# Decay exponents spread by loads and a predicated copy; x, B and the modulation sums turned by VectorE blocks

## The reference, cut to what matters

```python
acs = jnp.cumsum(a, axis=2)                       # a = dt * A, per chunk and head
seg = acs[:, :, :, None] - acs[:, :, None, :]
decay = jnp.exp(jnp.where(lower, seg, -jnp.inf))
cb = jnp.einsum('bclgn,bcsgn->bclsg', cm, bm)
y_diag = jnp.einsum('bclsg,bclsgr,bcsgrp->bclgrp', cb, decay, xdt)
...
mod_l = (jax.nn.silu(c) @ w_ada[layer] + b_ada[layer])[:, None, :]
```

## Time and profile before

| | us |
|---|---|
| median of 3 runs | 1884.4 (1882.55 to 1885.38) |
| the profiled execution, its own time | 1884.75 |
| span of the profiled execution | 1882.9 |

### The profile page before, as it was taken

The page is one execution under the profiler, slowest core; times in us unless marked ns, Lnnn a source line. Parts: engine busy times, 40 slices in busy tenths (PEclk is TensorE's granted clock), DMA queues, the critical chain, the costliest instruction groups (busy, mean ns, idle before and its releaser), DMA issues.

```text
span 1882.9 us, 15679 instructions
## 1 busy us (share of the span) xinstructions
PE 1435.3 (76%) x4503; PEld 830.9 (44%) x4503; DVE 1451.5 (77%) x2808; ACT 547.1 (29%) x1558; POOL 855.5 (45%) x626
## 2 busy tenths in 40 slices
PE   7999999999878888887787677677655554655554
PEld 2565687788545555554454234334311111211111
DVE  1545359773797779888967898889989889898877
ACT  3100233432332334223322432233322222222222
POOL 0888410010454443443434455446656555555551
PEclk9999999999989988999889898779878777777876
DMA  9534311343999999999999999999999999999995
GB/s 382 192 147 152 116 65 55 108 176 135 379 393 421 422 421 421 422 421 422 420 421 420 385 399 421 421 423 421 421 421 422 420 422 422 422 422 421 422 422 246
DMA packets 91228, 652.52 MB, mean 347 GB/s; under 512 B 10494, under 2 KB 10886, under 8 KB 12806
## 3 DMA queue, kind: packets, MB, share of 16 engines
q0 software_dynamic: 76448, 555.78, 71.6%
q1 hardware_dynamic: 13808, 93.39, 12.5%
q10 hardware_dynamic: 887, 2.35, 0.3%
HBM read 649.37 MB, written 2.11 MB: 346 GB/s over the span
## 4 chain that ended last, share of the span: by engine, by line
DMA 41%; PE 28%; DVE 20%; issue 6%; ACT 4%; POOL 1%; SPq 0%; DVEq 0%; ACTq 0%; POOLq 0%
DMA arena<-in_peer_uv,arena 40%; PE bank L834 12%; DVE arena L2038 8%; PE bank L1135 4%; DVE arena L2074 4%; PE bank L1023 3%; DMA arena<-in_w_ada 2%; PE bank L871 1%; POOL arena L766 1%; PE bank L948 1%; PE bank L1056 1%; ACT arena L1475 1%; PE bank L974 1%; PE bank L960 1%; DVE arena L2001 1%
## 5 line engine op out<-in xcount | busy, mean ns | idle before, releaser
L766 POOL DMA_INDIRECT arena<-in_peer_uv,arena x512 | 698.1, 1363 | 732.4 <-DVE arena L2074 451.8
L1135 PE MATMUL bank<-arena,smalls 128*128 128x512 f32 x1036 | 660.2, 772 | 419.5 <-ACT smalls L1483 419.4
L2038 DVE CUSTOM_DVE_ANT_0 arena<-arena 128x1024 f32<-128x1024 f32 x512 | 619.1, 1222 | 153.5 <-DMA arena<-in_peer_uv,arena 152.1
L1135 PEld LDWEIGHTS bank<-arena,smalls 128*128 128x128 f32 x1036 | 218.4, 229 | 781.1 <-ACT smalls L1483 589.1
L2074 DVE SCALAR_TENSOR_TENSOR arena<-arena 128x1024 f32<-128x1024 f32 x247 | 315.7, 1278 | 38.9 <-ACT arena L1475 36.3
L834 PE MATMUL bank<-arena 128*128 128x256 f32 (+1 forms) x1216 | 332.0, 430 | 2.2 <-ACT arena L1200 1.5
L1470 ACT ACTIVATE arena<-arena 128x2 f32<-128x2 f32 x255 | 51.9, 203 | 924.7 <-DVE arena L2038 924.6
L834 PEld LDWEIGHTS bank<-arena 128*128 128x128 f32 x1216 | 232.9, 193 | 102.4 <-issue 77.6
L1475 ACT ACTIVATE arena<-arena 128x1 f32<-128x1 f32 x510 | 122.5, 287 | 8.5
L1078 PE MATMUL bank<-arena 128*128 128x256 f32 x480 | 108.8, 380 | 0.0
L1483 ACT ACTIVATE smalls<-ident,arena 128x128 f32<-128x128 f32 x259 | 103.6, 401 | 8.3
(11 more groups left out here) (275 smaller groups left out, 1320.9 us busy)
## 6 DMA issues: line engine op xcount, KB each, us to landing
arena<-in_w_in SPq DMA_DIRECT2D x40, 1024.0 KB, 7.7
arena<-in_w_ada POOLq DMA_DIRECT2D x16, 1024.0 KB, 5.1
arena<-in_w_out SPq DMA_DIRECT2D x16, 1024.0 KB, 9.3
arena<-in_peer_w_q SPq DMA_DIRECT2D x16, 1024.0 KB, 9.3
arena<-in_w_ada SPq DMA_DIRECT2D x8, 1024.0 KB, 12.1
arena<-in_peer_uv,arena POOLq DMA_INDIRECT x512, 19.6
arena<-in_x SPq DMA_DIRECT2D x4, 512.0 KB, 11.9
arena<-in_x_t SPq DMA_DIRECT2D x1, 2048.0 KB, 16.0
```

The source lines that it names most:

```text
L766: nc.gpsimd.indirect_dma_start(gslot[slot], None, uv_tab[0], bass.IndirectOffsetOnAxis(eid[t % 2][:, k:k + 1], 0)).then_inc(s_gsl[slot], 16)
L1135: last = mm(acc[h][:, :], diag[:, k % NDG], row_v(n)[:, h * 512:(h + 1) * 512], start=first, stop=last_one)
L2038: V.tensor_tensor_reduce(row_u(n), row_u(n), h2[t], 1.0, 0.0, ALU.mult, ALU.add, dots[:, k:k + 1]).then_inc(s_dot, 1)
```

## The change

Four things are changed together:

- The exponents. The cumulative sums of the latent chunks are also computed transposed ("acsT": two matmuls, heads on the partitions), copied by ScalarE (`acsr`) and stored to a scratch in DRAM. For each block a load issued from ScalarE's queue spreads the 2 x 512 values of its heads over all 128 partitions (`load_rows`, three buffers `drows`). ScalarE then adds the negated sum of each partition's own token (`log_decays`, again eight instructions, in place), VectorE picks one direction or the other by a predicated copy of 128x512 at the start of `dt_times_cb`, and ScalarE takes the exponential from SBUF. `decay_sums`, its bank and its strict triangles are gone.
- x and B. The 72 transposes on TensorE and their drains are gone. VectorE turns 32x32 blocks from SBUF to SBUF (`turn_blocks`): for every pair of channel tiles 16 instructions on 32 partitions, of 256 elements for the latents and 128 for the context, 192 in all. They are put between the convolutions by `TURN`; the context part of the last three pairs follows after the last convolution, ahead of the dt chain.
- The modulation sums. `ada_sum` is gone; `ada_piece` is a VectorE reduction of 512 elements with a transpose, after every second channel tile, and one matmul by a folding matrix follows after the first z product. GpSimd waits for that reduction where it waited for TensorE. The bias is added by four instructions in place of eight small ones.
- The order. "acsT", "acs" and "m2T" stand between the third and the fourth z product, where they stood after the transposes.

```diff
-        if ct % 2 and ct > 1:
-            plan.append(("ada2", ct // 2 - 1))
-    plan += ["dtl", "dtc", ("ada2", NXB // 2 - 1), ("z", 0, 0), "dt"]
-    plan += [("z", hq, 0) for hq in range(1, 4)]
-    plan += [("xsT", m, h) for m in range(NT) for h in range(2)] + [("bT", m) for m in range(NT)]
-    plan += ["acs", "m2T"]
+    plan += ["dtl", "dtc", ("z", 0, 0), "dt", "ada2"]
+    plan += [("z", 1, 0), ("z", 2, 0), "acsT", "acs", "m2T", ("z", 3, 0)]
...
-        atri = [at(k, HPG * P) for k in (100, 102, 188, 190)]
+        drows = [at(k, 2, HPG * P) for k in (100, 48, 188)]
+        NDR = len(drows)
...
+        NBLK = P // 32
+        apart, fold = at(157, 4 * KD * NBLK), at(157.5, P)
...
-                    await_filled(pool, ("ada2", g - 2))
+                    pool.wait_ge(s_ared, g - 1)
...
+                    ps = claim("ada2")
+                    pe.wait_ge(s_fold, 1)
+                    pe.wait_ge(s_ared, NXB // 2)
+                    filled(mm(ps[:, 0:P], fold, apart, start=True, stop=True), "ada2")
+                if hq == 2:
+                    pe.wait_ge(s_a, 1)
+                    pe.wait_ge(s_const, 4)
+                    ps = claim("acsT")
+                    mm(ps[0:LT * HEADS, 0:P], adec[:, 0, 0:LT].rearrange("p m h -> p (m h)"), upper[:],
+                       start=True, stop=True)
+                    filled(mm(ps[0:LT * HEADS, P:2 * P], adec[:, 1, 0:LT].rearrange("p m h -> p (m h)"), lower[:],
+                              start=True, stop=True), "acsT")
+                    ps = claim("acs")
+                    NSC = NT * HEADS
+                    ad = adec[:].rearrange("p d m h -> p (d m h)")
+                    mm(ps[:, 0:NSC], upper[:], ad[:, 0:NSC], start=True, stop=True)
+                    mm(ps[:, NSC:2 * NSC], lower[:], ad[:, NSC:2 * NSC], start=True, stop=True)
+                    filled(mm(ps[:, 2 * NSC:4 * NSC], ones[:], ad, start=True, stop=True), "acs")
+                    pe.wait_ge(s_mod2, 1)
+                    filled(tr(claim("m2T")[0:4 * KD, 0:P], mod2[:], ident[:]), "m2T")
...
-            await_read(pe, ("bT", NT - 1))
+            pe.wait_ge(s_xtr, N_XTR)
...
-            def decay_sums(mg):
-
-                m, g = mg
-                b = m * NG + g
-                ps = claim(("r", m, g))
-                if b == 0:
-                    pe.wait_ge(s_tri, 4)
-                for d, tri in enumerate((after, before)):
-                    pe.wait_ge(s_atri, (2 * b + d + 1) * HPG)
-                    last = mm(ps[:, :], tri, atri[(2 * b + d) % 4], start=(d == 0), stop=(d == 1))
-                filled(last, ("r", m, g))
...
+            ps = await_bank(act, "acsT")
+            release(A(acsr[0:LT * HEADS].rearrange("p d t -> p (d t)"), ps[0:LT * HEADS, 0:2 * P], ACT.Copy), "acsT")
+            await_read(act, "acsT")
+            act.dma_start(acs_scratch.rearrange("d r t -> r d t"), acsr[0:LT * HEADS]).then_inc(s_acsst, 16)
+            z_gate(3)
+
+            def load_rows(b):
+                act.dma_start(drows[b % NDR], acs_scratch.rearrange("d (b r) t -> d b (r t)", r=HPG)[:, b]
+                              .partition_broadcast(P)).then_inc(s_drow[b % NDR], 16)
+
+            act.wait_ge(s_acsst, 16)
+            load_rows(0)
+            load_rows(1)
...
-                if b == 1:
-                    await_filled(act, ("st", len(steps) - 1, 1))
-                if b >= 2:
-                    await_filled(act, ("r", (b - 2) // NG, (b - 2) % NG))
-                for d, tri in enumerate((upper, lower)):
-                    dst = atri[(2 * b + d) % 4]
+                act.wait_ge(s_drow[b % NDR], 16 * (b // NDR + 1))
+                if b == 0:
+                    act.wait_ge(s_neg, 1)
+                for d in range(2):
                     for r in range(HPG):
-                        h = g * HPG + r
-                        A(dst[:, r * P:(r + 1) * P], tri[:], ACT.Copy, scale=adec[:, d, m, h:h + 1]).then_inc(s_atri, 1)
+                        row = drows[b % NDR][:, d, r * P:(r + 1) * P]
+                        A(row, row, ACT.Identity, bias=adec[:, d, m, g * HPG + r:g * HPG + r + 1]).then_inc(s_ldec, 1)
...
-                    ps = await_bank(act, ("r", m, g))
-                    if b >= 2:
-                        act.wait_ge(s_m, b - 1)
-                    release(A(decay[:, b % 2], ps[:, :], ACT.Exp), ("r", m, g))
-                    if b == 0:
-                        log_decays(1)
+                    act.wait_ge(s_ldsel, b + 1)
+                    A(drows[b % NDR][:, 0], drows[b % NDR][:, 0], ACT.Exp).then_inc(s_dexp, 1)
                     if b + 2 < LT * NG:
-                        log_decays(b + 2)
+                        if b == 0:
+                            await_filled(act, ("st", len(steps) - 1, 1))
+                        else:
+                            act.wait_ge(s_m, b)
+                        load_rows(b + 2)
+                    if b + 1 < LT * NG:
+                        log_decays(b + 1)
...
+            dve.wait_ge(s_const, 1)
+            V.tensor_reduce(out=fold.rearrange("p (a c) -> p a c", a=NBLK),
+                            in_=ident[:].rearrange("p (a c) -> p c a", a=NBLK).unsqueeze(1).to_broadcast([P, NBLK, 32, NBLK]),
+                            axis=mybir.AxisListType.X, op=ALU.add).then_inc(s_fold, 1)
+
             def ada_piece(g):
-                ps = await_bank(dve, ("ada2", g))
-                j = B_BA + 2 * KD + 4 * g
-                release(V.tensor_tensor(modr[:, 4 * g:4 * g + 4], ps[:, 0:4], colB[:, j:j + 4], ALU.add),
-                        ("ada2", g))
-
+                dve.wait_ge(s_asum, g + 1)
+                V.tensor_reduce(out=apart[:, 16 * g:16 * g + 16], in_=asum[:, g % 2].rearrange("p (b r) -> p b r", r=32),
+                                axis=mybir.AxisListType.X, op=ALU.add, apply_transpose=True).then_inc(s_ared, 1)
+
+            def turn_blocks(pair, ctx):
+
+                dve.wait_ge(s_xb, 4 * pair + 4)
+                src = xbc_c if ctx else xbl
+                ct = 2 * pair
+                dst, col = (xs, ct * P) if ct < NX else (Bt, (ct - NX) * P)
+                lo, hi = (LT, NT) if ctx else (0, LT)
+                for a in range(NBLK):
+                    for b in range(NBLK):
+                        i = src[32 * a:32 * a + 32, ct:ct + 2].rearrange("p k (m t) -> p k m t", t=P)
+                        o = dst[32 * b:32 * b + 32, lo:hi, col:col + 2 * P].rearrange("p m (k c) -> p k m c", c=P)
+                        V.transpose(o[:, :, :, 32 * a:32 * a + 32], i[:, :, :, 32 * b:32 * b + 32]).then_inc(s_xtr, 1)
+
+            TURN = {ct: [(ct // 2 - 1, 0)] for ct in range(3, NCTX + 2, 2)}
+            TURN |= {NCTX: [(0, 1)], NXB - 2: [(1, 1)], NXB - 1: [(2, 1)]}
...
+            ada_piece(NXB // 2 - 1)
+            for pair in range(3, NCTX // 2):
+                turn_blocks(pair, 1)
...
+            ps = await_bank(dve, "ada2")
+            for q in range(NBLK):
+                lanes = slice(32 * q, 32 * q + 32)
+                add = V.tensor_tensor(modr[lanes, :], ps[lanes, 0:P].rearrange("p (i q) -> p i q", q=NBLK)[:, :, q],
+                                      colB[lanes, B_BA + 2 * KD:B_BA + 6 * KD], ALU.add)
+                if q < NBLK - 1:
+                    post(add)
+            release(add, "ada2")
...
+            V.tensor_scalar(adec[:], acs[:], -1.0, None, ALU.mult).then_inc(s_neg, 1)
...
+                dve.wait_ge(s_ldec, 2 * HPG * (b + 1))
+                to_end, to_start = (drows[b % NDR][:, d].rearrange("p (r l) -> p r l", l=P) for d in range(2))
+                V.copy_predicated(to_end, lower[:].bitcast(U32).unsqueeze(1).to_broadcast([P, HPG, P]),
+                                  to_start).then_inc(s_ldsel, 1)
...
-                await_read(dve, ("r", m, g))
+                dve.wait_ge(s_dexp, b + 1)
                 settle()
-                V.tensor_tensor(mdec[:, b % 2], mdec[:, b % 2], decay[:, b % 2], ALU.mult).then_inc(s_m, 1)
```

More of the change, by code:

```diff
@@ L835, in project_T @@
                 filled(last, name)
-            def ada_sum(g):
-                ps = claim(("ada2", g))
-                pe.wait_ge(s_asum, g + 1)
-                for j in range(4):
-                    last = mm(ps[:, j:j + 1], asum[:, g % 2, j * P:(j + 1) * P], ones[:, 0:1],
-                              start=True, stop=True)
-                filled(last, ("ada2", g))
             for n in range(XBC // WCOL):
@@ L863, in _ @@
                 filled(last, name)
-            ada_sum(NXB // 2 - 1)
             def z_part(hq, half, i):
@@ L985, in y_transpose @@
                     filled(last, ("yT", m, h))
-            parts = {"proj": proj, "step": step, "cb": c_times_b, "r": decay_sums, "y": diagonal, "off": entering,
+            parts = {"proj": proj, "step": step, "cb": c_times_b, "y": diagonal, "off": entering,
                      "yT": y_transpose}
@@ L1221, in _, with z_gate @@
             A(alog[:], alog[:], ACT.Exp).then_inc(s_dtl, 1)
```

(2 more changed lines are left out.)

73 lines of the change are left out of this document (17 added, 56 removed).

## The result

| | median, us | runs from | to |
|---|---|---|---|
| before, 20 runs | 1883.5 | 1881.24 | 1886.45 |
| changed, 20 runs | 1889.38 | 1884.4 | 1893.95 |
| ratio | 1.0029 | 1.0023 | 1.0036 (95%) |

The changed kernel is 5.9 us slower. So the two traces show 1.9 of the 5.9 us, and what they don't show is taken up at the end.

What follows compares the result with a forecast made beforehand. TensorE, with VectorE as second limit, was taken to bound the part before the gathers, which DMA holds. Terms -9.3, +3.2 and -5.7 made -11.8 us: 1873.0 profiled, 1872.6 median; forecast 1868 to 1879, range 1863 to 1889.

Steps and rivals of the forecast that it cites:

- Price of a transpose: VectorE's block transposes ahead of the states: 0.22 us for 128 elements, 0.35 for 256, putting dt at 227.2 us.
- The rest of the front: From dt to the first state step: log decays, sums 1.3 us, fourth z 7.0, projection 3.5; step at 248.3.
- GpSimd, store and reload, exponentials of the sums at nothing: Ahead of the first state step: these lie beside other work and add nothing; exponentials some 3 us if uncovered.
- Stretch 2: First state step to second block of chunk 1: five predicated copies on a full VectorE, +3.2 us.
- Stretch 3: Second block of chunk 1 to entering states of the last chunk: VectorE paces at 79.1 us, 5.7 us sooner.
- the 4 us of new waits: VectorE's added waits in the later blocks, for ScalarE's loop and TensorE's last application: 4 us, between 0 and 10.
- The row loads: Loads of the sums in the blocks: landing in 4.8 us; rival of late landing decides from 10 us, chance 0.07.
- The sum: Whole kernel: -9.3 + 3.2 - 5.7 = -11.8 us, giving 1873.0 us profiled and a median of 1872.6.
- Each small instruction pays its full duration or a little more: Rival on VectorE's transposes: 0.28 to 0.31 and 0.41 to 0.44 us, costing 7 to 12 us; chance 0.17.
- From +0.1 us per instruction on the gain is eaten: VectorE's transposes behind channel tile 11: 0.1 us more each and the tail eats all of the 11.8 us.
- Two cycles per element: Rival on VectorE's transposes: 0.62 and 0.35 us each, 25 us more, 1898 us in all; chance 0.13.
- the estimate of no gain: From the skill page: transposes at 0.31 and 0.44 us lengthen the tail after channel tile 11 by 11.5 us.

Runs made afterwards that it cites:

- the turns late: Changed kernel with the last 48 of the 96 context transposes moved behind the dt chain and the copies of the sums; 1890.48 us, ratio 1.0038.
- four tiles a turn: Changed kernel with the same elements turned four channel tiles at a time, 96 instructions in place of 192; 1874.1 us, ratio 0.9948.
- the left-out kernel: Changed kernel with 48 of the 96 context transposes left out, so some values differ from the reference; 1869.23 us, ratio 0.9927.
- the version that beats both: Changed kernel with latents turned in 48 instructions of 512 elements and 24 context transposes back on TensorE between second and third z; 1870.31 us, ratio 0.9932.
- the second trace: Changed kernel run again, nothing edited, for another profile; median 1889.85 us, ratio 1.0024, profiled execution 1892.49 us.

## Why the prediction was wrong

- *Price of a transpose: the step that failed.* It took 0.22 and 0.35 us, "near the quick end", from pairs of L1784. Measured 0.333 and 0.464. With 96 and 32 of them behind channel tile 11 that is 96 x 0.113 + 32 x 0.114 = 14.5 us. Up to tile 11 the forecast held (VectorE free at 177.3, measured 177.31; that it is exact is luck, since five other traces with the same work up to there have 176.0 to 179.1), and from there dt came 14.7 late: 241.90 for 227.2. Two points give the law that the prediction lacked: 0.20 us + 1.02 ns per element. The slope was right (it had 1.04), the fixed part was not (0.07). The prediction reasoned that a step is shorter than the duration of one, as with L1784 (0.60 for 0.69). For these transposes it is longer: 0.333 for a mean duration of 0.301, and 0.464 for 0.433. Which of their differences from L1784 does it (the operation, the 32 partitions) no run tells.
- *The rest of the front.* The chain from dt to the log decays took 9.5 (9.2 predicted). The sums took 2.9 (251.43 to 254.34) for 1.3, and the fourth z 7.3 for 7.0: together 1.9 us, which the prediction priced at the full clock though it had itself put an idle TensorE ahead of them. The granted clock was 0.50 in the sums and 0.94 in the fourth z. At 1.00 the sums take 1.6, so 0.3 of it is a short count and not the clock. 14.7 + 0.3 + 1.9 = 16.9; the first step was forecast for 248.3 and came at 265.1.
- *A wait that it did not name.* The fold needs VectorE's last reduction; it had this at 216 and it came at 225.29 (the end of the reductions and turns, late for the same price). Ahead of it stands the wait of 4.12 us for ScalarE, which the prediction did not name either. The second and third z products stand behind both. In the changed kernel that was covered by the later wait of 8.49; in the kernels with dt early it comes to the fore (4.34 us with the turns late, 6.75 with four tiles a turn).
- *GpSimd, store and reload, exponentials of the sums at nothing:* no sign against it; the left-out kernel comes to 250.0 without a term for them. GpSimd's last sum does hold up VectorE's last reduction there, by 0.93 us, and by 5.31 in the version that beats both, but TensorE waits for neither.
- *Stretch 2:* +3.2 predicted, +2.9 measured (265.11 to 340.00, where before took 72.0). It counted five predicated copies up to this mark and eleven behind it; there are six and ten, the sixth at 339.38, so 0.6 us belong to the other stretch and the sum doesn't change. The copies step at 0.63, for 0.65:

```profile
339.38 0.73 DVE L1773 COPY_PREDICATED arena<-early,arena 128x512 f32<-128x512 uint32 x1
340.00 1.28 DVE L1784 TENSOR_TENSOR arena<-arena,smalls 128x512 f32<-128x512 f32 x2
```

- *Stretch 3:* -5.7 predicted, -8.1 measured. The mechanism was right, the 4 us of new waits were too many: they come to 1.6 us. VectorE's waits, 340 to 412 us, beside the earlier trace rows:

```profile
DVE arena L1794 <- DVE arena L1590: 0.5, 1, 0.5
DVE arena L1744 <- PE bank L822: 0.4, 1, 0.4
DVE arena L1764 <- PE bank L905: 0.3, 1, 0.3
DVE arena L1803 <- PE bank L918: 0.2, 1, 0.2
DVE arena L1773 <- ACT arena L1259: 0.2, 1, 0.2
```

- *The row loads.* The rival is out. They land in 4.8 us as taken, and ScalarE waited for them twice, 1.4 us in all (waits, 265 to 417 us):

```profile
arena<-acs_scratch ACTq DMA_DIRECT2D x16, 512.0 KB, 4.8
...
ACT arena L1259 <- DMA arena<-acs_scratch: 1.4, 2, 1.2
```

- *The sum.* 1873.0 + 16.8 (front) - 0.3 - 2.4 (blocks) = 1887.1, and the profiled execution took 1886.6. The median's further 2.8 us are not settled: the second trace shows its own 5.9 us ahead of the gathers and partly ahead of TensorE's first wait, and filling TensorE's waits won nothing clear of it.
- *The rivals.* "Each small instruction pays its full duration or a little more" was the one that happened, 0.02 us beyond its upper end (0.33 and 0.46, for 0.28 to 0.31 and 0.41 to 0.44); its 1880 to 1884 was too low by that and by those 1.9 us, while the blocks gained more than forecast. "From +0.1 us per instruction on the gain is eaten" was right as well. It was given 0.17, with a reason but no row for it; the row against it was of another operation and shape. Two cycles per element is out: the slope is that of L1784.
- The Trainium skill, "VectorE: DVE Perf Modes", sections "The three transpose paths" and "The TRN2 errata", had pointed the right way, against the change: small tiles pay a fixed extra per instruction. The trace agrees: 96 instructions fewer saved 16.1 us. Its 311 ns for a 128x128 bf16 transpose would have given the estimate of no gain; measured were 0.333 us for each 32x128 instruction, of which a 128x128 transpose takes four, and the time came out worse than that estimate.

## What to carry to other kernels

Price many small instructions from a row of the same partitions and size, and if there is none take a fixed part per instruction from the slow end: count times fixed part is what decides (here 128 x 0.11 us ate a gain of 12), and don't take a step shorter than the duration without a row of that operation. When work moves to another engine, ask first what is queued behind the wait that it makes late: with the same late dt chain the kernel took 11 us more with a z product behind it than with the product ahead. And the same transposes need not all go one way; those that fill an engine's waits may stay where they are.

## What the runs showed of the hardware

- A block transpose of float32 on 32 partitions steps at 0.333 us for 128 elements and 0.464 for 256, and at 0.731 for 512; 0.20 us fixed and 1.02 ns per element. The step is some 0.03 us longer than the mean duration (0.301, 0.433, 0.700).
- A reduction with transpose of 128x512 lasts 0.70 us, a predicated copy of 128x512 0.74 and steps at 0.63.
- TensorE's clock after its waits: "acsT", "acs" and m2T took 2.9 us at a granted clock of 0.50 (1.2 GHz) after waits of 8.49, 4.91 and 3.68 us, and 1.6 us at 1.00 (2.4 GHz) after one of 2.05, 0.61 or none. A projection after an idle 10.46 us took 4.93 (261.39 to 266.32, granted 0.71 on average) in place of 3.46.
